# Ten landing places for expert weights, low parts in place, and short blocks' products ahead of the first block's

## The reference

```python
def moe_swiglu(h, w_router, wg, wu, wd):
    logits = (h @ w_router).astype(jnp.float32)
    top_v, top_i = lax.top_k(logits, TOP_K)          # TOP_K = 2
    top_w = jax.nn.softmax(top_v, axis=-1)
    gates = jnp.einsum('blk,blke->ble', top_w, jax.nn.one_hot(top_i, N_EXPERTS, dtype=jnp.float32)).astype(h.dtype)
    y = jnp.zeros_like(h)
    for e in range(N_EXPERTS):                       # 8 experts, hidden width 1792
        y = y + gates[..., e:e + 1] * swiglu(h, wg[e], wu[e], wd[e])
    return y
```

## Time and profile before

| | before |
|---|---|
| median of 3 runs | 1368.78 us |
| profiled execution, its own time | 1364.29 us |
| its span, first to last instruction | 1362.1 us |
| granted TensorE clock, mean of the span | 0.973 of 2.4 GHz |
| PE busy | 1284.8 us (94%) |
| DVE busy | 719.4 us (53%) |
| ACT busy | 525.8 us (39%) |
| HBM read | 306 MB, 232 GB/s over the span |
| expert products run from, to | 746 us, 1337 us |

### The profile page before, as it was taken

The page is one execution under the profiler, slowest core; times in us unless marked ns, Lnnn a source line. Parts: engine busy times, 40 slices in busy tenths (PEclk is TensorE's granted clock), DMA queues, the critical chain, the costliest instruction groups (busy, mean ns, idle before and its releaser), DMA issues.

```text
span 1362.1 us, 17268 instructions
## 1 busy us (share of the span) xinstructions
PE 1284.8 (94%) x6503; PEld 958.8 (70%) x6504; DVE 719.4 (53%) x1026; ACT 525.8 (39%) x632; POOL 119.1 (9%) x119
## 2 busy tenths in 40 slices
PE   5999999999999989999999999999789999999994
PEld 2555459999999954677448886644357778888882
DVE  1101556243343345554337976523335769898898
ACT  0101034242332342142206653522324658777772
POOL 0510004000000051000000100101000010202020
PEclk8999999999999999999998899999999999999997
DMA  9985484434243184710407865778976879999993
GB/s 366 359 336 217 152 295 157 155 125 152 92 142 135 48 325 129 292 35 1 170 1 263 298 229 199 247 260 300 342 261 231 324 279 388 368 378 389 369 350 154
DMA packets 125355, 317.09 MB, mean 233 GB/s; under 512 B 12931, under 2 KB 47078, under 8 KB 124774
## 3 DMA queue, kind: packets, MB, share of 16 engines
q1 hardware_dynamic: 119264, 295.00, 59.0%
q0 software_dynamic: 5744, 21.07, 4.9%
q10 hardware_dynamic: 278, 0.10, 0.0%
HBM read 306.37 MB, written 9.76 MB: 232 GB/s over the span
## 4 chain that ended last, share of the span: by engine, by line
PE 83%; DMA 8%; DVE 4%; ACT 2%; SPq 2%; issue 1%; DVEq 0%; ACTq 0%
PE ps L2547 10%; PE ps L2549 9%; PE ps L2548 9%; PE ps L2245 8%; PE ps L2247 8%; PE ps L2246 8%; PE ps L2210 7%; PE ps L2147 6%; PE ps L2553 5%; DMA sb_expert_raw<-in_moe_w_up 4%; PE ps L2337 3%; DMA sb_ring<-in_ev_w_in 2%; PE ps L2107 2%; PE ps L2439 1%; DVE sb_expert_w L1765 1%
## 5 line engine op out<-in xcount | busy, mean ns | idle before, releaser
L1765 DVE TENSOR_TENSOR sb_expert_w<-sb_expert_raw,sb_expert_w 128x1792 fp32r<-128x1792 f32 (+1 forms) x210 | 338.6, 1648 | 118.0 <-ACT sb_expert_w L1214 117.1
L1214 ACT CAST sb_expert_w<-sb_expert_raw 128x1792 fp32r<-128x1792 f32 (+1 forms) x210 | 287.8, 1393 | 175.2 <-DMA sb_expert_raw<-in_moe_w_down 85.3
L2547 PE MATMUL ps<-sb_expert_w,sb_expert_x 128*128 128x448 f32 x448 | 170.8, 381 | 17.6 <-DVE sb_expert_w L1765 15.6
L2548 PE MATMUL ps<-sb_expert_w,sb_expert_x 128*128 128x448 f32 x448 | 168.4, 376 | 0.0
L2549 PE MATMUL ps<-sb_expert_w,sb_expert_x 128*128 128x448 f32 x448 | 168.2, 375 | 0.0
L2245 PE MATMUL ps<-sb_split_acts,sb_split_weights 128*128 128x384 f32 x352 | 118.7, 337 | 0.4 <-issue 0.4
L2247 PE MATMUL ps<-sb_split_acts,sb_split_weights 128*128 128x384 f32 x352 | 118.6, 337 | 0.0
L2246 PE MATMUL ps<-sb_split_acts,sb_split_weights 128*128 128x384 f32 x352 | 118.3, 336 | 0.0
L2547 PEld LDWEIGHTS ps<-sb_expert_w,sb_expert_x 128*128 128x128 f32 x448 | 87.2, 195 | 36.7 <-issue 27.2
L2549 PEld LDWEIGHTS ps<-sb_expert_w,sb_expert_x 128*128 128x128 f32 x448 | 87.2, 195 | 7.9
L2548 PEld LDWEIGHTS ps<-sb_expert_w,sb_expert_x 128*128 128x128 f32 x448 | 87.3, 195 | 7.6
(11 more groups left out here) (339 smaller groups left out, 1810.7 us busy)
## 6 DMA issues: line engine op xcount, KB each, us to landing
sb_expert_raw<-in_moe_w_gate SPq DMA_DIRECT2D x128, 448.0 KB, 5.6
sb_expert_raw<-in_moe_w_up SPq DMA_DIRECT2D x128, 448.0 KB, 7.3
sb_expert_raw<-in_moe_w_down SPq DMA_DIRECT2D x112, 512.0 KB, 7.0
sb_ring<-in_ada_w SPq DMA_DIRECT2D x14, 3072.0 KB, 17.1
sb_ring<-in_ffn_w_gate SPq DMA_DIRECT2D x44, 256.0 KB, 3.8
sb_ring<-in_ffn_w_up SPq DMA_DIRECT2D x44, 256.0 KB, 4.5
sb_ring<-in_ffn_w_down SPq DMA_DIRECT2D x22, 512.0 KB, 6.3
sb_ring<-in_ev_w_in SPq DMA_DIRECT2D x4, 2048.0 KB, 14.9
```

The source lines that it names most:

```text
L1214: nc.scalar.copy(EWS[r][:, 0, 0:w], ERAW[:, r, 0:w]).then_inc(e_hi, 1)
L1765: V.tensor_tensor(EWS[r][:, 1, 0:w], ERAW[:, r, 0:w], EWS[r][:, 0, 0:w].bitcast(F32), ALU.subtract)\
L2547: first = mm(out, lh, rh, start=start, stop=False)
L2548: mm(out, lh, rl, start=False, stop=False)
```

## The change

- The landing places go from six to ten (`ESLOTS`). The low part is written over the raw piece, in its landing place (`ELO` lies on `ERAW`); only the high part has a place of its own (`EHI`, `HSLOTS` = 6). The places moved: the scratch region and the region of the transposed hidden rows are laid out anew, and the last sums are loaded into scratch (`YG`).
- A landing place is free again only when PE has used the piece, in every pass: piece n waits for piece n-10. ACT still waits for piece n-6.
- In passes 1 and 3 the raw piece must be used before its low part covers it. PE does the second block's first four pieces ahead of the first block's, and stays ahead; DVE makes the low part only after the second block's product (`second_used`). SiLU, hidden product, transposes and copies of the second block come before those of the first.
- At the start SP loads ten pieces in place of six ahead of the three stores of token rows.

```diff
-ESLOTS = 6
+ESLOTS, HSLOTS = 10, 6
...
             def expert_free(piece):
-                if isinstance(piece.n, int) and piece.n < ESLOTS:
-                    return
-                if piece.prior_split is None:
+                if not (isinstance(piece.n, int) and piece.n < ESLOTS):
                     sp.wait_ge(e_used, piece.n - (ESLOTS - 1))
-                else:
-                    sp.wait_ge(e_lo, piece.prior_split + 1)
...
-            for c in range(3, ESLOTS):
+            for c in range(3, 6):
                 expert_gate_up(e_piece(0, c), 0, 0, c)
+            sp.wait_ge(used[2], ring.used[2])
+            for c in range(6, ESLOTS):
+                expert_gate_up(e_piece(0, c), 0, c // KD, c % KD)
...
-                if not (isinstance(n, int) and n < ESLOTS):
-                    act.wait_ge(e_used, n - (ESLOTS - 1))
+                if not (isinstance(n, int) and n < HSLOTS):
+                    act.wait_ge(e_used, n - (HSLOTS - 1))
                 w = 2 * EW if kind == "g" else D
-                nc.scalar.copy(EWS[r][:, 0, 0:w], ERAW[:, r, 0:w]).then_inc(e_hi, 1)
+                nc.scalar.copy(EHI[piece.h][:, 0:w], ERAW[:, r, 0:w]).then_inc(e_hi, 1)
...
                 dve.wait_ge(e_hi, piece.split + 1)
-                V.tensor_tensor(EWS[r][:, 1, 0:w], ERAW[:, r, 0:w], EWS[r][:, 0, 0:w].bitcast(F32), ALU.subtract)\
+                if piece.mixed is not None:
+                    dve.wait_ge(second_used, piece.mixed + 1)
+                V.tensor_tensor(ELO[r][:, 0:w], ERAW[:, r, 0:w], EHI[piece.h][:, 0:w].bitcast(F32), ALU.subtract)\
                     .then_inc(e_lo, 1)
...
                 select(after)
-                expert_lows(p, 4, KD + 4)
+                expert_lows(p, 4, KD)
+                if p in SECOND:
+                    second_hidden(p, 0)
+                expert_lows(p, KD, KD + 4)
                 hidden(p, 0)
...
-                expert_lows(p, turn, 2 * KD + EB + 4)
-                hidden(p, 1)
+                expert_lows(p, turn, 2 * KD + EB)
+                if p in SECOND:
+                    second_hidden(p, 1)
+                    expert_lows(p, 2 * KD + EB, 2 * KD + EB + 2)
+                    hidden(p, 1)
+                    expert_lows(p, 2 * KD + EB + 2, 2 * KD + EB + 4)
+                else:
+                    expert_lows(p, 2 * KD + EB, 2 * KD + EB + 4)
+                    hidden(p, 1)
...
+                ahead = 4 if more_rows else 0
+                for k in range(ahead):
+                    secondary(k)
                 for k in range(0, KD, 2):
                     primary(k)
                     primary(k + 1)
-                    if more_rows:
-                        secondary(k)
-                        secondary(k + 1)
+                    if more_rows and k + ahead < KD:
+                        secondary(k + ahead)
+                        secondary(k + ahead + 1)
...
+                if more_rows:
+                    for j in range(4):
+                        secondary(j)
+                hidden_split(pe, p, u, 0)
                 for j in range(spread(p)):
                     primary(j)
                 between()
                 if more_rows:
-                    for j in range(spread(p)):
+                    for j in range(4, EB):
                         secondary(j)
-                for j in range(spread(p), EB, 2):
-                    pair = range(j, min(j + 2, EB))
-                    for i in pair:
-                        primary(i)
-                    if more_rows:
-                        for i in pair:
-                            secondary(i)
+                for j in range(spread(p), EB):
+                    primary(j)
```

More of the change, by code:

```diff
@@ L65 @@
 CANDS = 3 * NE
-Piece = namedtuple("Piece", "n r land whole split prior_split")
+Piece = namedtuple("Piece", "n r h land whole split mixed")
 class Rows:
@@ L118 @@
 WHOLE = [p for p, (_, b, _) in enumerate(PASSES) if b.streams > 1]
-KEPT = SECOND + WHOLE
-assert not {NS - 1, 0} & set(KEPT)
+assert not {NS - 1, 0} & set(SECOND + WHOLE) and all(p + 1 not in SECOND for p in SECOND)
 SPREAD = {1: 3, 2: 5}
@@ L449, in build @@
         FF_LAST = pieces.take(1)
+        expert_in = [sem(f"expert_in{r}") for r in range(ESLOTS - 4)] + raw_in[:4]
+        EXPERT_BASE = [0] * (ESLOTS - 4) + pieces.landed[:4]
         FIRST_KINDS = "g" * KD + "g" * KD + "d" * EB
@@ L495, in piece_before, with before_of @@
[L495 to L515, removed]
+        def before_of(passes, p, c):
+            n = 0
+            for q in passes:
+                if not isinstance(p, int) or p > q + 1:
+                    n += ITEM_N
+                elif p == q:
+                    n += sum(owner(q, d) == q for d in range(c))
+                elif p == q + 1:
+                    n += ITEM_N - EB + sum(owner(p, d) == q for d in range(c))
+            return n
@@ L538, in units_seen @@
         def units_seen(p, u, second=0):
-            return nth(p, 2, 2 * second_before(p) + u * (2 if blocks_of(p)[1] else 1) + second)
+            both = blocks_of(p)[1]
+            return nth(p, 2, 2 * second_before(p) + u * (2 if both else 1) + (3 - second if both and second else second))
         def split_seen(p, a):
@@ L1265, in y_out @@
                 w = D // b.streams
[L1266 removed]
+                act.wait_ge(yd, seen(p, 2 if more_rows else 1))
                 if p != 0:
@@ L2554, in each_stream, with gate_up_block @@
                 return made[0], made[-1]
-            def gate_up_block(b, x, r, k):
-                first = None
+            def gate_up_block(b, x, piece, k):
+                first, r, hi = None, piece.r, piece.h
                 cols = slice(k * b.n, (k + 1) * b.n)
@@ L2612, in secondary @@
                         hidden_split(pe, p, 0, 1)
-                    _, last = gate_up_block(more_rows, XES2, e_piece(p, c0 + k).r, k)
-                    last.then_inc(gu_ps if k == KD - 1 else e_used, 1)
+                    piece = e_piece(p, c0 + k)
+                    pe.wait_ge(expert_in[piece.r], piece.land)
+                    first, last = gate_up_block(more_rows, XES2, piece, k)
+                    if owed and k == 0:
+                        first.then_inc(e_used, 1)
+                    last.then_inc(second_used, 1)
+                ahead = 4 if more_rows else 0
+                for k in range(ahead):
+                    secondary(k)
                 for k in range(0, KD, 2):
@@ L2647, in primary @@
                     piece_ready(pieces[j])
-                    first, last = down_block(b, h, b.home(j), pieces[j].r, first_of and j == 0, last_of and j == EB - 1)
-                    if owed and j == 0:
+                    first, last = down_block(b, h, b.home(j), pieces[j], first_of and j == 0, last_of and j == EB - 1)
+                    if owed and j == 0 and not more_rows:
                         first.then_inc(e_used, 1)
-                    if last_of and j == EB - 1:
-                        last.then_inc(yd, 1)
-                    elif not more_rows:
-                        last.then_inc(e_used, 1)
+                    if more_rows and last_of and j == spread(p):
+                        first.then_inc(yd, 1)
+                    last.then_inc(yd if last_of and j == EB - 1 else e_used, 1)
                 def secondary(j):
```

151 lines of the change are left out of this document (73 added, 78 removed).

## The result

Four runs of the changed kernel have a median of 1337.12 us (1334.6 to 1338.61) beside 1369.65 us (1368.09 to 1371.23) for four of the kernel before: a ratio of 0.976, 95% interval 0.974 to 0.978. The prediction was 1337.4 us in a range from 1330 to 1354. The profiled run took 1337.3 us; its span is 1335.4 us, the mean clock 0.975.

The account below looks back on a forecast made before the run. Six landing places, not PE or the transfers, were taken to bound the kernel from pass 1 until the pure half passes; 37.2 - 4.8 - 2.3 + 1.3 = 31.4 us gain, from 1368.8 to 1337.4 us, range 1330 to 1354.

Parts of the forecast that it names:

- the stretches from B to R: Groups of pieces in PE's order, from pass 1 to the pure half passes; hardly one keeps full pace.
- Waits gone, 37.2 us: Pass 1 until the pure half passes: ten places can end all waits over full-pace work, 37.2 us in sum.
- F, I with J and L: Stretches ahead of the pure half passes, 2.5, 11.8 and 5.3 us over their full-pace work, 19.6 together.
- its four bare times: Full-pace work of the last four stretches before the pure half passes: 15.1, 19.5, 14.5 and 19.5 us.
- 16 us to spare from F0 to K3, each piece landed 3 us or more ahead: Mixed passes and pass 2: 25.7 MB take 67 us at 383 GB/s, wanted 83 us later, so transfers fit.
- New waits, 4.8 us: Mixed passes: low parts waiting for `second_used` delay DVE's queue; 4.8 us lost, bounds 1.5 and 16.
- One clock drop, 2.3 us: After a new wait the granted clock falls once, 2.3 us lost; bounds none and four drops of up to 3.1.
- Ten where there were twelve: nothing: Pure passes: places held until PE is done; a 13.3 us stay fits the 20.5 us of ten pieces, no loss.
- the slower rival: Pure half passes: ten places too few, deciding from a 14.4 us landing; at 19 us, 48 us lost, 1380; chance 0.07.
- Start: zero: Start of expert products: four more loads ahead of the token-row stores cost nothing, as DVE needs the stores 10 us later.
- End: 1.3 us: After the last products: SP's last piece is issued earlier, so DVE's gate rows come sooner; gain 1.3 us, bounds 0 and 2.5.
- The median: The 31.4 us gain taken from the median 1368.8 gives 1337.4 us; from the profiled execution's 1364.3 it gives 1332.9.

Follow-up runs that it names:

- both repeats: The changed kernel, unchanged, profiled and timed again twice, beside later experiments: medians 1335.7 us (ratio 0.975) and 1337.2 us (0.976).
- the run with both edits: Changed kernel with all seven second-block products ahead of the first block's and pass 1's accumulating scatters held back: median 1330.1 us, ratio 0.971.

## Why the prediction was right, and where it wasn't

The main mechanism was right: too few places, and not PE or the transfers, held up the stretches from B to R. That the time came out within 0.3 us of the forecast is luck on top of it, since terms missed by 1 to 4 us both ways.

- *Waits gone, 37.2 us.* Right in each place but K: F, I with J and L gained 19.7 us where 19.6 stood. Reading each stretch against the same work elsewhere at full pace was the step that carried the forecast, and the run with seven products ahead met three of its four bare times to 0.1 us (the fourth, N, is 0.3 shorter).
- *16 us to spare from F0 to K3, each piece landed 3 us or more ahead.* Wrong, and it cost 3.6 us of waiting in K. The sum took the pieces alone, at 383 GB/s. In the changed kernel F, H, and I with J show 358, 334 and 350 GB/s over all queues at a DMA share of 0.97 or more; 25.7 MB at 350 are 73 us, not 67, and E, which the sum counts in full, ran at a share of 0.83. POOL's gathers and scatters took 23% of the engines between 940 and 965 us and stood in no term: the pieces got 7.18 MB through there, 287 GB/s. K3 had been named as the place with the least cover; that was right, and no price was put on it. (A slip beside it changes nothing: 22.0 MB at 383 to 408 GB/s are 54 to 57 us, not 55 to 58.)
- *New waits, 4.8 us.* The places were right, O0 and R0 with 1.26 and 1.19 us (forecast 3.3 together), N and Q. Undoing them gave 5.1 us in N to R (73.4 to 68.3) and 5.6 to 6.6 in the whole stretch, so the size was right too, with some of it in gaps that no semaphore wait shows. That K and M would wait 0.5 us isn't seen.
- *One clock drop, 2.3 us.* In the first profile none came: 1.00 in every stretch from A to R, behind waits of up to 1.26 us. In both repeats one came, in K, at 0.95 over some 33 us, so 1.6 us lost. The count was right for two profiles of three, the size a little high, and the place wrong: it stands behind the waits for landings at K0 to K2, which the sum didn't have, and not behind a wait for a low part. Waits of at most 1.2 us, in a row, were thus followed by it in two executions and not in a third. The Trainium skill (TensorE: Matmul & The Clock Gate, HAM oscillation) tells of a kernel that falls to the lower clock at every one of its recurring waits for transfers, which are 3 to 5 us long there. The traces agree that waits for transfers can cost the clock, though these were shorter, and differ in that at most one fall came in a row of three or four.
- *How the terms offset each other.* In the first profile K came out 3.65 us worse than the sum and N and Q 1.5 and 1.6 worse; the clock came out 2.3 us better, A, C and E, which stood at zero, 1.4, O and R 1.25 and 1.35, and the six half passes 1.2.
- *Ten where there were twelve: nothing.* Right; the six half passes even gained 1.2 us. The way of working it out was sound, its number for the longest landing was not: the earlier trace rows had 9.8 us, the repeat of the kernel before has 12.2 and the changed kernel 13.6, with a median of 7.5 against 7.1. With 13.6 us the stay is 13.6 + 1.69 + 2.02 + 2.4 = 19.7 us, and ten pieces last 20.5. So 0.8 us were to spare and not 4.5, and the slower rival was nearer than its case against it, those 9.8 us, made it look; the run with eight places, where the same sum gives 20.2 against 16.4, lost 4.6 us in its half passes.

```profile
DMA to landing us min/median/max: 3.9/7.5/13.6
```

- *Start: zero.* Right, though the first pair of traces seemed to refute it by 5.5 us; the kernel before shows both starts. The changed kernel's own three profiles are all of the late kind; two versions of it with edits only in later stages started early, at 746.5 and 748.0 us.
- *End: 1.3 us.* From the last product to the end of the span it was 25.4 us and is 24.2, a gain of 1.2. The last piece is issued 13.8 us before the end of the products, against 11.6 before.
- *The median.* Taking the gain from the median, and not from the profile's own time, was worth 4.5 us: the profile of before was an early starter.

## What to carry to other kernels

Set every stretch against the same work elsewhere in the same trace at full pace; the differences sum to what deeper buffering can give, and a busy share of 90% hides them. When a buffer's depth changes, count the stay with the landing that a piece has while other queues' transfers run beside it, not with the median, and put those transfers into the rate: here they fell on the place with the least cover. A work-around that forces an order (here: raw products ahead of low parts) should be pushed as far as it goes, seven ahead rather than four, if what it leaves behind sits at the tail of another engine's queue.

## What the runs showed of the hardware

- POOL's accumulating scatters cost the DMA engines more than their bytes. In the changed kernel 1.44 MB of gathers and scatters took 23.0% of the engines in 25 us, and 7.18 MB of pieces 77.1%. With the scatters moved away, in the run with both edits, the gathers' 0.66 MB took 6.9% of the window from 940 to 965 us, as much by the byte as the pieces (95.6% for 9.39 MB). That leaves 16.1% for 0.78 MB of scatters, about twice as much by the byte; it is a difference of two windows. The median landing of an up half had been 11.7 us. The Trainium skill (DMA: Bandwidth & Descriptors, SWDGE vs HWDGE vs iDMA) says that each DMA engine takes turns between the queues of the two kinds; that agrees with pieces being slowed and not only displaced, but no run here separates turns from bytes.
- Waits for landing pieces of at most 1.2 us each, three or four in a row (in the first repeat 1.06, 1.09 and 1.18 us), stood before a fall of the granted clock in two profiles of one kernel; in a third, waits of 1.15, 1.11 and 1.21 us left it at 1.00.
- The clock from 722 to 746 us, PE busy for about 22 of 24 us or more, was 0.57 in one profile of the kernel before and 0.79 in the other. Over all twelve profiles the expert products started at 746.4 to 748.0 us with 0.79 and at 752.0 to 754.8 us with 0.57 to 0.61, so two single profiles can't be compared by their ends.
